# Attention with the probabilities stationary and the values moving, and the query rotation moved to GpSimd

## The reference

```
def blocked_attention(q, k, v):
    ...
        s = jnp.einsum('bqkgd,bskd->bkgqs', qblk, k).astype(jnp.float32) * scale
        p = jax.nn.softmax(s, axis=-1).astype(v.dtype)
        return jnp.einsum('bkgqs,bskd->bqkgd', p, v)
```

## Time and profile before

| | |
|---|---|
| time, median of 3 runs | 3112.44 us (3108.32 to 3116.27) |
| span of the profiled execution | 3114.3 us |
| PE busy / PEld busy | 2989.0 us (96%) / 2463.1 us (79%) |
| DVE / ACT / POOL busy | 1929.1 / 995.1 / 403.8 us |
| attention walk, first layer: first `scores_T` to the first product of the output projection | 405.07 to 654.98 us |

### The profile page before, as it was taken

The page is one execution under the profiler, slowest core; times in us unless marked ns, Lnnn a source line. Parts: engine busy times, 40 slices in busy tenths (PEclk is TensorE's granted clock), DMA queues, the critical chain, the costliest instruction groups (busy, mean ns, idle before and its releaser), DMA issues.

```text
span 3114.3 us, 43652 instructions
## 1 busy us (share of the span) xinstructions
PE 2989.0 (96%) x16207; PEld 2463.1 (79%) x16207; DVE 1929.1 (62%) x3490; ACT 995.1 (32%) x1948; POOL 403.8 (13%) x582
## 2 busy tenths in 40 slices
PE   6999989999999999999979998999999999999998
PEld 5787844567899899988968887454788999889997
DVE  4547777745776677766575577777467444554447
ACT  3322345535221222211353233445261221212212
POOL 1012333411000000000020033433010000000002
PEclk8999989999999999999989999999999999999999
DMA  7331210012132223322121111100212010111102
GB/s 290 122 124 42 72 62 0 0 50 69 63 109 63 73 82 108 95 68 91 33 99 56 33 52 60 61 0 27 72 41 68 28 55 28 55 41 41 54 28 75
DMA packets 93846, 201.45 MB, mean 65 GB/s; under 512 B 12432, under 2 KB 13088, under 8 KB 93024
## 3 DMA queue, kind: packets, MB, share of 16 engines
q1 hardware_dynamic: 78240, 151.76, 15.0%
q0 software_dynamic: 15424, 47.25, 4.4%
HBM read 181.88 MB, written 17.08 MB: 64 GB/s over the span
## 4 chain that ended last, share of the span: by engine, by line
PE 56%; issue 29%; DVE 7%; DVEq 2%; DMA 2%; ACT 1%; POOL 1%; POOLq 1%; SPq 0%; ACTq 0%
PE ps L1947 12%; PE ps L1951 12%; PE ps L1950 12%; PE ps L2199 6%; PE ps L2189 3%; PE ps L2190 2%; PE ps L2169 2%; DMA w_raw<-in_w_slots 1%; PE ps L2078 1%; DMA modw<-in_w_mod 1%; DVE xr L1736 1%; DVEq L1735 1%; DVE w_lo L532 1%; PE ps L1929 1%; PE ps L2035 1%
## 5 line engine op out<-in xcount | busy, mean ns | idle before, releaser
L1947 PE MATMUL ps<-hi,w_hi 128*128 128x384 f32 x1536 | 515.1, 335 | 4.0 <-DVE w_lo L532 4.0
L1951 PE MATMUL ps<-hi,w_lo 128*128 128x384 f32 x1536 | 513.4, 334 | 0.0
L1950 PE MATMUL ps<-lo,w_hi 128*128 128x384 f32 x1536 | 513.2, 334 | 0.0
L527 ACT CAST w_hi<-w_raw 128x512 fp32r<-128x512 f32 x368 | 215.0, 619 | 758.2 <-PE ps L1947 676.7
L1947 PE MATMUL ps<-w_hi,hi 128*128 128x512 f32 (+1 forms) x1008 | 394.2, 391 | 12.7 <-ACT stg L865 5.5
L1950 PE MATMUL ps<-w_lo,hi 128*128 128x512 f32 (+1 forms) x1008 | 384.1, 381 | 0.0
L1951 PE MATMUL ps<-w_hi,lo 128*128 128x512 f32 (+1 forms) x1008 | 383.9, 381 | 0.0
L1776 DVE TENSOR_TENSOR ps<-ps,gate 128x512 f32<-128x512 f32 x288 | 201.0, 698 | 238.2 <-PE ps L1951 238.1
L1947 PE MATMUL ps<-w_hi,f_hi 128*128 128x512 f32 x864 | 337.4, 391 | 8.3 <-DVE xr L1779 4.3
L1951 PE MATMUL ps<-w_hi,f_lo 128*128 128x512 f32 x864 | 336.9, 390 | 0.0
L1950 PE MATMUL ps<-w_lo,f_hi 128*128 128x512 f32 x864 | 336.9, 390 | 0.0
(11 more groups left out here) (319 smaller groups left out, 4805.8 us busy)
## 6 DMA issues: line engine op xcount, KB each, us to landing
w_raw<-in_w_slots SPq DMA_DIRECT2D x368, 256.0 KB, 3.2
w_raw<-in_m_slots SPq DMA_DIRECT2D x160, 256.0 KB, 3.0
out<-xr POOLq DMA_DIRECT2D x18, 512.0 KB, 3.2
modw<-in_w_mod SPq DMA_DIRECT2D x4, 2048.0 KB, 15.5
acc<-in_x_in SPq DMA_DIRECT2D x3, 1536.0 KB, 16.2
zq_dram<-stg POOLq DMA_DIRECT2D x18, 256.0 KB, 2.3
xr<-in_x_in POOLq DMA_DIRECT2D x2, 2304.0 KB, 10.6
xr<-out POOLq DMA_DIRECT2D x2, 2304.0 KB, 10.7
```

Source lines behind the costliest of these rows:

```text
L527: act.copy(w_hi[:, j, :], w_raw[:, j % RAW, :]).then_inc(S["w_hi_done"], 1)
L1947: mm = pe.matmul(out, a_hi, b_hi, start=first, stop=False)
L1950: pe.matmul(out, a_hi, b_lo, start=False, stop=False)
L1951: return pe.matmul(out, a_lo, b_hi, start=False, stop=last)
```

## The change

The values now move and the probabilities stand still. For key tile j and head h, `values` loads the 128x128 block of `pr[:, j]` as stationary operand and moves the 65 columns of `vst` (64 values and a one) through it. The result has queries in rows, with the sum over keys in column 64, so that there is nothing to transpose and nothing to add up apart. The passes of the values are spread over the step, two key tiles behind `scores_T` (`LAG`). `pairs`, `ninth`, `row_sums`, `outputs_T`, `sums_T`, their copies on ScalarE and the additions on GpSimd go. `outputs` on VectorE becomes a reciprocal and a multiplication. VectorE only norms the queries; GpSimd rotates and doubles them. `queries(1, 0)` moves ahead of the walk, and each step norms the block three ahead. `shift` moves to the end of the step.

```diff
-SCORES_AT = {1: 1, 3: 2, 6: 3}
-PREP = ((0, 1), (), (2,), ())
+SCORES_AT = {1: 0, 3: 1, 5: 2, 6: 3}
+LAG = 2
...
-        vst = put("vst", [HKV, 10, HD])
+        vst = put("vst", [HKV, 10, VE])
```

GpSimd loses the additions (`added`, not repeated here) and gains the rotation of the block three ahead:

```diff
                 def step(t, g, nk, pk, nn, prep):
+                    G, E = counts(L, t, g)
+                    for h in range(HG if nn else 0):
+                        diagonal(G, g, h)
+                    if prep is not None:
+                        rotated(G + 3, *prep)
+
+                def rotated(G, t, g):
+
+                    pool.wait_ge(S["qn_done"], G + 1)
+                    a, h_ = slice(g * HG, g * HG + HG), HD // 2
+                    o_ = qn[:, 0:HG * HD].rearrange("p (a b) -> p a b", b=HD)
...
+                    for r in range(2):
...
+                        pool.tensor_tensor(d4, q4[:, :, ::-1, :], spread(s4, HG), ALU.mult)
+                    pool.tensor_tensor(qd[:, a, 0], o_, spread(rope_of(t, 0), HG), ALU.mult)
+                    pool.drain()
+                    pool.tensor_tensor(qd[:, a, 0], qd[:, a, 0], qd[:, a, 1], ALU.add)
+                    pool.drain()
+                    pool.tensor_copy(qd[:, a, 1], qd[:, a, 0]).then_inc(S["qd_done"], 1)
```

ScalarE loses its two copies in each step:

```diff
-                        if pk > 1 and j == min(1, nk - 1):
-                            values_out(G - 1, B)
-                            sums_out(G - 1, B)
```

VectorE divides at once, and its queries are cut to part 0 (`normed`):

```diff
+                def outputs(t, g, E, bank):
+
+                    dve.wait_ge(S["pv_done"], START + E)
+                    o4 = ps[:, bank, 0:HG * VE].rearrange("p (a b) -> p a b", b=VE)
+                    dve.reciprocal(rinv[:, g], o4[:, :, HD])
+                    dve.drain()
+                    dve.tensor_tensor(zq[:, t, g * 256:g * 256 + 256].rearrange("p (a b) -> p a b", b=HD), o4[:, :, 0:HD],
+                                      b2(rinv[:, g], HD), ALU.mult).then_inc(S["oy_done"], 1)
...
                     for h in range(HG if nn > 1 else 0):
                         maximum(G + 1, 1 - g, h, nn)
-                        if prep is not None:
-                            queries(prep, g, PREP[h])
+                        if h == 0:
+                            before()
+                        if prep is not None and h == 1:
+                            dve.wait_ge(S["qd_done"], G + 3)
+                            queries(*prep, (0,))
```

TensorE has the values by key tile and a new order of the step:

```diff
+                def values(G, E, g, j, nk):
+
+                    pe.wait_ge(S["ex_done"], START + E + j + 1)
+                    if j == 0:
+                        pe.wait_ge(S["oy_done"], START + G - 1)
+                    for h in range(HG):
+                        mm = pe.matmul(ps[:, 5 + g, h * VE:(h + 1) * VE], pr[:, j if nk > 1 else g, h * P:(h + 1) * P],
+                                       vst[:, g, j if nk > 1 else NT], start=(j == h == 0), stop=(j == nk - 1 and h == HG - 1))
                     mm.then_inc(S["pv_done"], 1)
...
                     for j in range(nk):
                         scores_T(G, E, g, j, nk, pk)
+                        if pk > 1 and nk > 1 and j < LAG - 1:
+                            values(G - 1, E - pk, 1 - g, pk - LAG + 1 + j, pk)
+                        elif nk > 1 and j >= LAG:
+                            values(G, E, g, j - LAG, nk)
...
+                        if nn > 1 and j in SCORES_AT:
+                            scores(G + 1, 1 - g, SCORES_AT[j], nn, pk)
...
+                    if nn:
+                        shift(G + 1, 1 - g)
+                    if nk > 1:
                         queries_T(G + 2, g)
+                    values(G, E, g, max(nk - LAG, 0), nk)
```

More of the change, by code:

```diff
@@ L1015, in values_in @@
                         c = v * HD
+                        act.copy(vst[:, v, :, HD:VE], ones[:, 0:10].unsqueeze(2))
                         act.copy(vst[:, v, 0:NS, 0:HD], z[:, 0:NS, P + c:P + c + HD])
@@ L2267, in step @@
-                        if pk > 1 and j == min(3, nk - 1):
-                            if nn:
-                                pe.wait_ge(S["q_lo_done"], START + G + 2)
-                            outputs_T(G - 1)
-                        if pk > 1 and j == min(5, nk - 1):
-                            sums_T(G - 1)
-                        for key, h in SCORES_AT.items():
-                            if nn > 1 and j == min(key, nk - 1):
-                                scores(G + 1, 1 - g, h, nn, pk)
@@ L2276, in step @@
-                        if nk > 1 and j == 6:
-                            for i in range(3):
-                                pairs(G, E, g, i)
-                        if nn and j == max(nk - 3, 0):
-                            shift(G + 1, 1 - g)
-                    if nn and prep is not None:
+                        if nn > 1 and j in SCORES_AT:
+                            scores(G + 1, 1 - g, SCORES_AT[j], nn, pk)
+                        if nn == 1 and j == min(1, nk - 1):
+                            scores_last(G + 1, 1 - g)
@@ L2282, in step @@
+                    if nk == 1 and pk > 1:
+                        values(G - 1, E - pk, 1 - g, pk - 1, pk)
+                    if nn:
+                        shift(G + 1, 1 - g)
+                    if nk > 1:
                         queries_T(G + 2, g)
+                    values(G, E, g, max(nk - LAG, 0), nk)
                 pe.wait_ge(S["m_read"], L + 1)
```

173 lines of the change are left out of this document (39 added, 134 removed).

## The result

The changed kernel took 3183.65 us in the median of four runs (3162.14 to 3194.77), the kernel before 3113.66 us beside it; the ratio is 1.0212 with a 95% interval of 1.0169 to 1.0256. It is slower by some 2%. The profiled execution is the fastest of the four, 3162.14 us. The four differ by 33 us, the four of before by 8 us, and the time goes with the mean granted clock of TensorE: 0.975, 0.971, 0.966 and 0.964 from the fastest to the slowest. That spread is the second thing to explain, beside the median.

What follows compares the result with a forecast made beforehand. Bound by what TensorE issues. Per layer 15 steps x 1.7 = 25.5, start +2, end -4: 23.5 us; two layers 47 us on 3114.3 give 3161.3, or 3159 us as median; range 3122 to 3194.

Steps and rivals of the forecast that it cites:

- The value record: Value products on PE: 72 records a step at 0.11 to 0.12 us, nine groups 7.7 us against 6.4 us removed.
- The step: Steady attention step on PE: 15.9 us, 1.7 us more than now, bounds 1.0 to 2.3.
- The start: Ahead of each layer's walk: one more query preparation on VectorE, 3.1 us, partly regained; +2 us, bounds -1 and +6.
- The end: Last-but-one pair to output projection: 16.26 us becomes 12.4, without two sums, two copies, eight transposes; gain about 4, bounds 0 and 6.
- eight hand-overs: Part of the chain at the walk's end: eight hand-overs at an estimated 0.2 us, within 7.7 us.
- Who could make PE wait: Other engines in a step: GpSimd's rotation 3.2 us, at most 6.4, with room for 9.9; costed at nothing.
- The remark on GpSimd's additions: Two-input VectorE operations contend with GpSimd for SBUF: 1.029 us beside additions, 0.426 with one such input without; slows `queries_lo`, unpriced.
- (a): Value records: weight loads hide beneath the record before, under 0.093 us each; faster, 3051 us; chance 0.07.
- (b): Steps: late `normed` delays the third and fourth maxima, PE waits 1 us in each of 30 steps; 3189 us; chance 0.14.
- (c): No change: step difference 0.3 us or less, paid for by the shorter ends; 3112 us; chance 0.07.
- (d): TensorE's granted clock falls in the walk, 30 steps at the lower level; +477 us, some 3640; chance 0.04.
- the mLSTM stretch: Argument against the clock falling in the walk: a stretch with the same record form in it kept 1.00.

Runs made afterwards that it cites:

- short filler: Changed kernel plus 12 unused products of 128 columns (24 records) ahead of the first score group of each layer's first step: 3196.45 us, ratio 1.0229.
- long filler: Changed kernel plus 16 unused products of 512 columns in the first step's wait, ahead of the second score group: 3140.40 us, ratio 1.0094.
- late preparation: Changed kernel with VectorE's preparation of the third block of queries moved from ahead of the walk to behind the first maximum: 3171.95 us, ratio 1.0190.

## Why the prediction was right, and where its sizes were not

The forecast was 3159 us, slower, in a range of 3122 to 3194; the median is 3183.65. Sign and main mechanism hold. The sum for the span of the profiled execution was 3161.3 us, and that span is 3159.9. That they are so near is luck: the forecast +47 us is 51 for the steps, +4 for the starts and -8 for the ends, the measured +45.6 is 36.8, +12.9 and -4.5, with 3.8 for the slow second step of layer 2 and -3.4 in the rest of the span. The execution is also the fastest of the four; the median lies 24 us above the forecast.

*The value record.* The step "Nine groups are 9 x 0.86 = 7.7 us" was right in kind and 6% too long. A record takes 0.81 / 8 = 0.10 us, below the 0.11 to 0.12 that I had named as the sign, and columns are worth next to nothing: 0.13 us a step from 65 to 128. The rows 0.81 against my 0.86 for a group show an overestimate of 9 x 0.05 = 0.45 us a step. The Trainium skill, "TensorE: Matmul & The Clock Gate", LDWEIGHTS, gives 107 ns for 128 columns of weights, whatever the number of rows. The trace agrees at the higher clock (0.10 us); for 64 columns the short filler's 0.115 us a record doesn't follow that count.

*The step.* Predicted +1.7 us (bounds 1.0 to 2.3), measured 216.55 / 14 - 14.2 = +1.25. Per layer fourteen of them give 17.5 us, and with the shorter step ahead of the last pair 18.4, where I had 25.5.

*The start.* The term of the sum that failed: "Bounds -1 and +6 us; I take +2." The wait for the first maximum did not grow (4.51 us, before 4.63), yet the first step took 6.2 and 6.7 us longer, outside the bounds. I saw the clock of 0.69 in the earlier trace rows and priced the added preparation alone, not what the lower clock does to a step that now has five or six value groups behind the wait to run at it, at 1.56 in place of 0.81 us each. With the clock held the term is 20.54 - 22.15 = -1.6 us (long filler), and 18.90 - 22.15 = -3.3 with the late preparation.

*The end.* Predicted -4, to a stretch of 12.4 us; measured 13.46 and 14.56 us in the profile, at a clock of 0.75 and 0.65, and 11.47 us at 1.00 in both layers of the kernel with 128 columns. With the clock up the chain was sized within 1 us, though its eight hand-overs of 0.2 us came from no row and were not measured singly; the rest goes with the clock.

*Who could make PE wait.* Right: no gap on PE in the steady steps, GpSimd's rotation 2.8 us where I had 3.2, and worth nothing in the steady step by itself (rotation on VectorE: the same step). The remark on GpSimd's additions misread a row: the operation of 0.426 us, `zq<-zq,rinv`, has both inputs in SBUF too, but no addition ran beside it. `queries_lo`, which I expected to be slowed, took 0.68 us in both traces.

*The rivals.* (a) fell: a record takes 0.10 us, above the 0.093 at which it would decide, with 65 columns as with 128. (b) fell for the changed kernel. (c) fell. (d), to which I gave 0.04 and 3640 us, is true in part: the clock does fall, not for all thirty steps but for the first of each layer and up to a whole second one, and by the mean clocks this separates the median from the profiled run. With 33 columns, and with 66 in fp32r, it came true for the whole walk. My argument against it, the mLSTM stretch, looked at a stretch at 1.00 from end to end. It shows that such records can run at the higher level, not that they bring a clock back that has fallen. With the long filler sixteen steps take 250.40 and 250.03 us, 16.8 and 16.6 more than before, and the ends 13.89 and 13.05, 2.4 and 3.2 less: 27.8 us together, and the median is 27.5 us above before. In these ends the clock fell once more (a value group of 1.97 us at the end of layer 1). From there to the two medians of the changed kernel are 43 and 33 us. The profiled executions, 22 us apart in span, show 21 of them in the walk and its end; for the others only the mean clock speaks.

What stays open is when exactly the clock falls and returns: the changed kernel took from part of a step to two steps for the return, and the short filler seven in its longest execution.

## What to carry to other kernels

Before counting multiplications, count the records that load weights of their own: each took 0.1 us here at the higher clock, whether 65 or 128 columns moved, and a float32 product is two of them. (With 512 columns moving, a record took 0.23 us, as the twelve at 508.14 in the earlier trace rows.) The operand that is reused belongs in the array. Where records become short, look at the granted clock of every step, not only of the steady ones, and at several executions: a spread that goes with the mean clock is the sign. If a wait brings the clock down, shorten it or put long records into it, and try wider records, which from 65 to 128 columns cost almost the same here and brought it back sooner.

## What the runs showed that was not expected

- A TensorE without a gap was granted the lower clock for fifteen steps on end: 422.02 us busy of 422.02 at 0.50 with 33 columns, and 306.82 of 306.82 at 0.50 with 66 columns of fp32r. With 65 columns of float32 it had a whole step of that kind with the late preparation, 27.76 us busy of 27.76 at 0.51. The Trainium skill, "TensorE: Matmul & The Clock Gate", Part 1, calls the lower level that of an idle engine. By the busy time of the profile the trace does not agree, and the measurement decides: a busy PE is no evidence of the higher clock.
- The price of a record is tied to that clock: a group of eight records took 0.81 us at the higher level and 1.56 at the lower, each with a pair behind it (with 33 columns and a score group behind it 1.68, 502.06 to 503.74).
- Useless work paid: against the two medians of the changed kernel, 128 columns in place of 65 took off 36 and 26 us, and 16 unused products 43 and 33 us.
